# Expert loop of a two-layer trunk: the gathered rows turned at the head of a pair's own iteration, its two first products one behind the other

## What is computed

```python
# hf: 512 x 1024 normed tokens; each goes to 2 of 32 experts with a gate
xb = hf[buf_tok]                                     # rows gathered, sorted by expert, in blocks
yb = (silu(xb @ w1[e]) * (xb @ w3[e])) @ w2[e]       # w1, w3: 1024 x 512, w2: 512 x 1024
y  = zeros.at[buf_tok].add(yb * buf_w[:, None])      # added back to the tokens, by the gate
```

## Time and profile before

| what | value |
|---|---|
| runs of the kernel, median of 3 | 1898.15 us (1897.12 to 1903.28) |
| profiled execution: span, first to last instruction | 1903.4 us |
| profiled execution: its own time | not given beside the span |
| mean granted TensorE clock | 0.990 of full speed |
| TensorE busy | 1864.9 us, 98% |
| VectorE, ScalarE, GpSimd busy | 571.7, 460.3, 170.3 us |
| chain that ended last | TensorE 80%, DMA 14%, VectorE 4% |
| expert loop of layer 0, first to last iteration's start | 574.79 to 998.03 us |
| the same of layer 1 | 1432.19 to 1853.22 us |

### The profile page before, as it was taken

The page is one execution under the profiler, slowest core; times in us unless marked ns, Lnnn a source line. Parts: engine busy times, 40 slices in busy tenths (PEclk is TensorE's granted clock), DMA queues, the critical chain, the costliest instruction groups (busy, mean ns, idle before and its releaser), DMA issues.

```text
span 1903.4 us, 21644 instructions
## 1 busy us (share of the span) xinstructions
PE 1864.9 (98%) x8098; PEld 930.9 (49%) x8098; DVE 571.7 (30%) x1040; ACT 460.3 (24%) x809; POOL 170.3 (9%) x207
## 2 busy tenths in 40 slices
PE   8999899999999999999999999999999999999998
PEld 4555898646463333333333443586463333333333
DVE  2154566442142313223133102311242313223132
ACT  3254243242331111111112003333331111111112
POOL 2000233030100000000001000031100000000000
PEclk9999799999999999999999999999999999999999
DMA  6210100035079999999996112204079999999994
GB/s 189 88 45 12 33 1 1 6 119 211 0 278 423 423 424 423 425 423 423 423 424 251 68 46 89 88 1 175 6 280 423 423 423 424 424 423 423 423 422 195
DMA packets 89133, 466.29 MB, mean 245 GB/s; under 512 B 22383, under 2 KB 24543, under 8 KB 48122
## 3 DMA queue, kind: packets, MB, share of 16 engines
q1 hardware_dynamic: 78176, 450.98, 58.4%
q0 software_dynamic: 4608, 7.92, 1.1%
q10 hardware_dynamic: 6298, 6.68, 1.1%
HBM read 468.12 MB, written 6.29 MB: 249 GB/s over the span
## 4 chain that ended last, share of the span: by engine, by line
PE 80%; DMA 14%; DVE 4%; ACT 1%; issue 1%; SPq 0%; DVEq 0%
PE ps L1048 73%; DMA W<-in_moe_w 14%; PE ps L1257 3%; PE ps L1749 1%; PE ps L1720 1%; PE ps L1644 0%; DMA xin<-in_x 0%; PE ps L1484 0%; PE ps L1683 0%; PE ps L1194 0%; DVE XI L2035 0%; DVE gcs L2138 0%; DVE XJ L1972 0%; DVE KKt L2005 0%; DVE gsn L2169 0%
## 5 line engine op out<-in xcount | busy, mean ns | idle before, releaser
L1048 PE MATMUL ps<-W,xgT 128*64 128x512 f32 x2048 | 454.4, 594 | 7.0 <-DMA W<-in_moe_w 5.8
L1048 PE MATMUL ps<-HT,W 128*128 128x512 f32 (+2 forms) x896 | 337.4, 533 | 3.7 <-DVE HT L1868 1.5
L1048 PEld LDWEIGHTS ps<-W,xgT 128*64 128x64 f32 x2048 | 143.4, 137 | 288.6 <-issue 270.9
L1048 PEld LDWEIGHTS ps<-HT,W 128*128 128x128 f32 (+1 forms) x896 | 166.4, 188 | 162.6 <-issue 151.2
L2297 DVE TENSOR_TENSOR XT<-ps,XT 128x512 f32<-128x512 f32 x240 | 166.0, 692 | 240.8 <-PE ps L1048 240.8
L1048 PE MATMUL ps<-W,act 128*64 128x512 f32 x1024 | 231.9, 595 | 0.0
L1048 PE MATMUL ps<-spread,ysb 128*128 128x512 f32 x496 | 221.1, 599 | 1.1 <-issue 1.1
L2289 DVE TENSOR_TENSOR act<-ps,sl 128x256 f32<-128x256 f32 x64 | 26.9, 420 | 445.4 <-ACT sl L1000 445.4
L1048 PEld LDWEIGHTS ps<-spread,ysb 128*128 128x128 f32 x496 | 91.7, 190 | 130.1 <-issue 129.9
L1048 PEld LDWEIGHTS ps<-W,act 128*64 128x64 f32 x1024 | 70.5, 137 | 133.4 <-issue 133.4
L996 ACT ACTIVATE hs<-ps 128x512 f32<-128x512 f32 x64 | 38.2, 597 | 389.0 <-PE ps L1048 389.0
(11 more groups left out here) (412 smaller groups left out, 1709.6 us busy)
## 6 DMA issues: line engine op xcount, KB each, us to landing
W<-in_moe_w SPq DMA_DIRECT2D x256, 1024.0 KB, 17.5
W<-in_moe_w SPq DMA_DIRECT2D x64, 2048.0 KB, 18.7
W<-in_od_w_in SPq DMA_DIRECT2D x6, 2048.0 KB, 8.3
W<-in_ev_w_in SPq DMA_DIRECT2D x3, 2048.0 KB, 7.7
W<-in_xa_wq SPq DMA_DIRECT2D x2, 2048.0 KB, 8.9
W<-in_xa_wo SPq DMA_DIRECT2D x2, 2048.0 KB, 12.0
hrows<-hk ACTq DMA_DIRECT2D x8, 512.0 KB, 11.1
W<-in_od_w_out SPq DMA_DIRECT2D x2, 2048.0 KB, 9.8
```

Source lines behind the costliest of these rows:

```text
L1048: return te.matmul(o, l, r, start=first, stop=last)
```

## The change

In the loop, pair i's rows are turned at the head of iteration i, not late in iteration i - 1. Then comes the second product of pair i - 1's block 1, then both first products of pair i one behind the other, then the turning of block 0's hidden rows, the addition, the turning of block 1's, and block 0's second product. Pair 0 has the order of before, less the turning for pair 1. The turning that fed no pair is gone. ScalarE, VectorE and SyncE take the new order; the bounds of the semaphores follow it. The diff, with its outer context cut:

```diff
 # SyncE
                 with sp.Fori(2, trips) as i:
+                    down(1, i - 1)
                     up(0, i)
-                    down(1, i - 1)
                     up(1, i)
                     down(0, i)
 # GpSimd
-                    pool.wait_ge(s["xg_turned"], i + (pairs + 1))
+                    pool.wait_ge(s["xg_turned"], i + (pairs + (1 - L)))
 # ScalarE
                 def pair_of_blocks(i, first=False):
-                    take_hidden(0, i)
                     if not first:
                         take_y(1, i - 1)
-                    gate_hidden(0, i)
-                    take_hidden(1, i)
+                    take_hidden(0, i)
+                    if first:
+                        gate_hidden(0, i)
+                        take_hidden(1, i)
+                    else:
+                        take_hidden(1, i)
+                        gate_hidden(0, i)
                     gate_hidden(1, i)
                     take_y(0, i)
...
+            act.wait_ge(s["gb_step"], trips + pairs)
 # TensorE
-                def pair_of_blocks(i, first=False):
+                def first_pair():
+                    up(0, 0)
+                    turn_hidden(0, 0)
+                    up(1, 0)
+                    turn_hidden(1, 0)
+                    down(0, 0)
+
+                def pair_of_blocks(i):
+                    pe.wait_ge(s["add_in"], i * 8 + pairs * 8)
+                    turn_rows(i * 16 + pairs * 16)
+                    down(1, i - 1)
                     up(0, i)
-                    if not first:
-                        down(1, i - 1)
+                    up(1, i)
                     turn_hidden(0, i)
-                    up(1, i)
-                    if not first:
-
-                        pe.wait_ge(s["y_in"], i * 2 + (pairs * 2 + 1))
-                        pe.wait_ge(s["spread_in"], i + pairs)
-                        add_pair(lambda k: pe.wait_ge(s["add_in"], i * 8 + (pairs * 8 + (k - 1))))
-                        pe.wait_ge(s["add_in"], i * 8 + (pairs * 8 + 8))
-                    turn_rows(i * 16 + (pairs * 16 + 16))
+
+                    pe.wait_ge(s["y_in"], i * 2 + (pairs * 2 + 1))
+                    pe.wait_ge(s["spread_in"], i + pairs)
+                    add_pair(lambda k: pe.wait_ge(s["add_in"], i * 8 + (pairs * 8 + (k - 1))))
                     turn_hidden(1, i)
                     down(0, i)
 # VectorE
                 def pair_of_blocks(i, first=False):
+                    if not first:
+                        take_rows(i + (pairs + (1 - L)))
                     gated(0, i)
...
-                    take_rows(i + (pairs + 2))
                     gated(1, i)
```

More of the change, by code:

```diff
@@ L1032, in _ @@
             cross(1)
-            moe(1, pairs)
+            trips = moe(1, pairs)
             st.then(sc.activation(xrs[:, 0:1], cst[:, 0:1], ACT.Sqrt))
+            act.wait_ge(s["gb_step"], trips + pairs)
             for t in range(TT):
@@ L1648, in last_rows @@
                 pe.wait_ge(s["add_in"], (trips + pairs) * 8 + 2)
-                pe.wait_ge(s["xgT_in"], trips + (pairs + 2))
+                pe.wait_ge(s["xgT_in"], trips + pairs)
                 turn_tokens(0)
@@ L1731, in up @@
                     if b == 0:
-                        pe.wait_ge(s["xgT_in"], i + (pairs + (L + 1)))
+                        pe.wait_ge(s["xgT_in"], i + (pairs + 1))
                     pe.wait_ge(wa_in[b], (i + 1) * 32 + pairs * 32)
@@ L1762, in down @@
                     ins.then_inc(s["y_done"], 1)
-                def pair_of_blocks(i, first=False):
+                def first_pair():
[8 more added lines that the diff above has]
+                    down(1, i - 1)
                     up(0, i)
-                    if not first:
-                        down(1, i - 1)
+                    up(1, i)
                     turn_hidden(0, i)
-                    up(1, i)
-                    if not first:
-                        pe.wait_ge(s["y_in"], i * 2 + (pairs * 2 + 1))
-                        pe.wait_ge(s["spread_in"], i + pairs)
-                        add_pair(lambda k: pe.wait_ge(s["add_in"], i * 8 + (pairs * 8 + (k - 1))))
-                        pe.wait_ge(s["add_in"], i * 8 + (pairs * 8 + 8))
-                    turn_rows(i * 16 + (pairs * 16 + 16))
+                    pe.wait_ge(s["y_in"], i * 2 + (pairs * 2 + 1))
+                    pe.wait_ge(s["spread_in"], i + pairs)
+                    add_pair(lambda k: pe.wait_ge(s["add_in"], i * 8 + (pairs * 8 + (k - 1))))
                     turn_hidden(1, i)
                     down(0, i)
-                pair_of_blocks(0, first=True)
+                first_pair()
                 pe.wait_ge(s["plan_v"], PLAN_V * (L + 1))
@@ L1799, in taken @@
                         pe.wait_ge(s["xt_ready"], n["xt"] + k - 3)
-                pe.wait_ge(s["xgT_in"], trips + (pairs + (L + 1)))
+                pe.wait_ge(s["xgT_in"], trips + pairs)
                 add_pair(taken)
```

## The result

The changed kernel takes **1907.19 us** (median of 7 runs, 1904.44 to 1911.52) against 1898.15 of the kernel before (7 runs, 1895.31 to 1903.28). The ratio is 1.0038 with a 95% interval of 1.0021 to 1.0056. Beside each other again, with 12 runs and 34, it was 1.0029 (1.0011 to 1.0048). So it is slower by 0.3 to 0.4%, and 0.1 to 0.6% if the intervals are taken in.

A forecast was written before the change was run, and what follows sets the result against it. TensorE was taken as the bound, busy 1864.9 of 1903.4 us, with 8.2 us of weight waits. To the median 1898.15 it added 3.4 from the layers and 2.5 for waits ordinary runs lack: 1904.0 us, range 1897 to 1910.

The forecast's parts named there:

- The iteration: TensorE's iteration in the expert loops goes from 29.86 to 30.25 us, 0.39 more.
- the two sums of 30.29 and 30.21: TensorE's new iteration added from differences of starts (30.29), or from bare work plus each change of width once (30.21).
- The new wait: At each iteration's head `down(1)` waits for ScalarE to empty bank 6: 0.35 us stall, bounds 0.25 and 0.5.
- Pair 0, "nothing": In pair 0 the turning of rows goes but comes back at the head of iteration 1: no gain.
- What the queue gives back: Slower iterations cost 11.5 us, 8.2 us of weight waits vanish into it; loops lose 3.4 us against the profile.
- From profile to runs: Span 5.25 us above the runs' median: 2.75 clock, 2.5 weight waits ordinary runs lack; runs lose 3.4 + 2.5 = 5.9.
- the 1909.7: Rival: ordinary runs hardly wait for weights, so nothing absorbs the 11.5 us; 1909.7 us, chance 0.12.
- the 1901.5: Rival: the weights' queue absorbs the stall in ordinary runs as in the profiled one; 1901.5 us, chance 0.24.
- The order of loads, "nothing": SyncE's w2 load of block 1 moves ahead of `up(0)`'s loads; given nothing, as a full queue lands each load the same.
- The rival without a stall: ScalarE's copies end under the turning of rows, so `down(1)` doesn't wait; 1896.7 us, chance 0.10.
- The clock: Rival: transposes and stall together drop TensorE to 1.2 GHz, `down(1)` 3.4 us longer in 30 iterations; about 2000, chance 0.02.

The follow-up runs named there:

- bank 3: Changed kernel with block 1's second product put in PSUM bank 3 instead of 6; runs -1.6 and -1.3 us against the kernel before at equal clock, ratios 0.9993 and 0.9997.
- the second profile of the kernel before: Kernel before, no edit, profiled again; its two loops took 949.12 us against 952.86 in the first profile.
- the copy in four: Kernel before with ScalarE's copy of block 0's second product in four pieces of 256 columns, not two of 512; ratio 0.9990 to the kernel before.
- the last experiment: Changed kernel with SyncE's loads in the old order, up(0) then down(1); loops 959.99 us, ratio 1.0031 to the kernel before.

## Why the prediction was right, point by point

- **The forecast**, 1904.0 us, was +5.9 on the median; measured were +6.1 +-0.9 at equal clock and 0.29 and 0.38% by the two ratios. The plain medians differ by 9.0 us in the first set and 6.0 in the second. The median of 1907.19 stands 3.2 above the forecast, within the range. That 5.9 and 6.1 lie so close is in part luck, as the next points show.
- **The iteration.** 30.25 us was forecast, between the two sums of 30.29 and 30.21, and measured. Two terms of the sum were off and cancel. The hand-over from ScalarE to TensorE, taken as 0.04 us from a case in pair 0, is 0.11 to the weights and 0.14 to the product, so `down(1)` starts 1.46 us after `turn_rows` and not 1.35. The addition between two transposes takes 627.38 - 620.51 = 6.87 and not 6.97.
- **The new wait** is there in all 30 iterations. The stall was put at 0.35 us, within 0.25 and 0.5; it is 0.43, by the start of `down(1)` with and without it (1.46 and 1.03), while the trace's rows say 0.36. That it is this wait and nothing else that costs is shown from both sides: removed by bank 3 (29.82), prolonged by 0.11 (30.37).
- **Pair 0, "nothing".** The number is right and the reason isn't. The turning at the head of iteration 1 is already in the 30.25, so by the forecast's own sum pair 0 should have become 0.87 us shorter in each layer. It didn't, because in the old order the turning covered ScalarE's copy to `hs`, and now `turn_hidden(1)` waits for that copy (before, then after):

```profile
570.78 0.60 PE L1749 MATMUL ps<-ident,hs 128*128 128x128 f32 x4
```
```profile
566.73 0.66 PE L1754 MATMUL ps<-ident,hs 128*128 128x128 f32 x4 [0.70 <-ACT hs L996]
```

  From `up(1)` of pair 0 to iteration 1 it is 11.96 us before and 11.95 after. A wait that was overlooked and a turning that was counted twice, 1.7 us over both layers, cancel: luck.
- **What the queue gives back.** In the profile the loops lost 3.3 us, forecast 3.4: by layer +0.53 and +2.81, forecast +0.57 and +2.79. The waits on weights are gone, as forecast. Against the second profile of the kernel before, 949.12, the same loops lose 7.1.
- **From profile to runs.** This was the weakest step, a split of 5.25 us into clock (2.75) and waits (2.5). Both exist, and neither has its size. The 5.25 set a span beside times: every later profiled run took 1.7 or 1.8 us more than its span, so the gap was about 7.0. And the median of 1898.15 was low, 3.7 below the median of the 77 later runs. The waits vary, 8.1, 4.4 and 7.2 us in three profiles (two of the kernel before, one with the copy in four; each against 944.74), and come to 6.8 +-1.1 in the runs, where the forecast had taken 8.2 - 2.5 = 5.7. With 1.3 in place of 2.5 the sum would have been 4.7 and not 5.9, against 6.1 +-0.9 measured; what makes up the rest, no run shows. Neither rival came true: no profiled execution of the kernel before went without waits, as the 1909.7 wanted (4.4 us was the least), and on average the queue gives back less than the 8.1 us of the first profile, which the 1901.5 had counted on.
- **The order of loads, "nothing".** For the kernel as changed this stands: no weight is late. The reason given, that a full queue gives each load the same landing whoever asks first, is incomplete. In the changed kernel each is asked for as soon as its buffer is free, and none is late. Asked for 8.6 us later, as in the last experiment, a load does land late, at 3.2 to 3.8 us in all.
- **The rival without a stall** said 1896.7, or 1.5 us below before. That is what the version with bank 3 does: -1.6 and -1.3 us. The queue of weights holds it there.
- **The clock** stayed at 1.00 in the loops. The Trainium skill ("TensorE: Matmul & The Clock Gate", section "Part 4: PE-mode transpose") says that transposes don't count as busy work in the way products do. Nothing of that showed here: 16 transposes an iteration (the prediction counts 12), the turned rows and a wait side by side never lowered the clock.
- **The rate of transfers.** The Trainium skill ("DMA: Bandwidth & Descriptors", section "Where 436 GB/s comes from") gives 435 GB/s for the ports into SBUF and says that for transfers from HBM a lower limit, about 358 GB/s, binds. The weights came at 421 to 425 GB/s in the full stretches of both kernels, under the first and above the second, so the second didn't bind here.

## What to carry to other kernels

When two products that share one PSUM bank move next to each other, count what lies between them against the copy that empties the bank: here 6.9 us shrank to 1.0, against 1.2 of copy and 0.26 of hand-overs before and behind it. A bank that is idle at that moment removed the wait at no cost. Where work is taken out, look for a copy of another engine that it had covered, as in pair 0. And where an engine's iteration and the queue's period lie as close as 29.86 and 30.36 us here, speeding up or slowing down the engine is worth only what the other doesn't hide; take the queue out (here by halving one load) to see the engine's own cost.

## What the runs showed of the hardware that was not expected

- Halving the pieces of a copy out of PSUM was nearly free: four ACTIVATEs of 64x256 took 1.31 us together against 1.20 for two of 64x512.
- After the wait on ScalarE at the head of an iteration, TensorE's weight load came 0.11 us after the copy's end and the product 0.14 after it in 29 of 30 iterations and 0.22 in one; in pair 0, where `hs` had been waited for, the load came 0.04 after it.
- Executions of one unchanged kernel wait between 4.4 and 8.1 us for the same weights, at the same 423 GB/s in the full stretches. What moves them by this much was not tried.
